# A two-block float32 network on one core: the first projection fed by blocks of 128 channels, seven units at once

## The reference

```python
c_act = jax.nn.silu(c)
mod = c_act @ ada_w[l] + ada_b[l]                 # [1, 6*1024]
sh1, sc1, g1, sh2, sc2, g2 = split(mod, 6)
h = rmsnorm(x, norm_mix_w[l]) * (1.0 + sc1) + sh1 # [512, 1024]
proj = h @ w_in[l]                                # [512, 3624]
(hq, hf, hi, hg, sq, sk, sv, iq, ik, iw, cu) = split(proj)
o_a = hgrn2_mixer(hq, hf, hi, hg, ...)            # recurrence over chunks
o_b = dsa_mixer(sq, sk, sv, iq, ik, iw)           # scores of iq, ik, iw; top 128 keys; attention
o_c = conv_module(cu, ...)                        # gate, convolution of 31 taps, layer norm
x = x + g1 * (concat(o_a, o_b, o_c) @ w_out[l])
```

## Time and profile before

| | us |
|---|---|
| median of three runs | 1356.24 |
| the profiled execution's own time | 1354.19 |
| its span | 1352.6 |
| PE busy | 1278.8 (95%) |
| DVE busy | 849.5 (63%) |
| ACT busy | 579.9 (43%) |
| POOL busy | 103.9 (8%) |
| mean granted clock of PE | 0.974 |

### The profile page before, as it was taken

The page is one execution under the profiler, slowest core; times in us unless marked ns, Lnnn a source line. Parts: engine busy times, 40 slices in busy tenths (PEclk is TensorE's granted clock), DMA queues, the critical chain, the costliest instruction groups (busy, mean ns, idle before and its releaser), DMA issues.

```text
span 1352.6 us, 18764 instructions
## 1 busy us (share of the span) xinstructions
PE 1278.8 (95%) x6581; PEld 1026.4 (76%) x6581; DVE 849.5 (63%) x1273; ACT 579.9 (43%) x820; POOL 103.9 (8%) x154
## 2 busy tenths in 40 slices
PE   6799788999899999999999999999999989999997
PEld 2677566878688788788888888787788877777776
DVE  4679798666765422344444787775366547887853
ACT  3366442651444211244333465332233335878731
POOL 7014330000000000000000000110011000000000
PEclk9799898998899999999999999999999999999999
DMA  8576982323544433333333223333222332333231
GB/s 295 149 209 134 201 167 70 111 78 124 157 140 132 132 93 93 86 101 93 93 93 94 69 87 86 90 91 106 84 87 81 98 93 70 87 90 92 59 94 62
DMA packets 209912, 147.88 MB, mean 109 GB/s; under 512 B 7682, under 2 KB 192177, under 8 KB 209856
## 3 DMA queue, kind: packets, MB, share of 16 engines
q1 hardware_dynamic: 200784, 134.40, 33.6%
q0 software_dynamic: 6848, 11.69, 4.9%
q10 hardware_dynamic: 2224, 1.05, 0.3%
HBM read 135.06 MB, written 2.10 MB: 101 GB/s over the span
## 4 chain that ended last, share of the span: by engine, by line
PE 69%; DVE 14%; issue 6%; DMA 5%; ACT 5%; POOL 1%; DVEq 0%; ACTq 0%; SPq 0%; POOLq 0%
PE banks L393 21%; PE banks L395 20%; PE banks L394 20%; ACT w_hi L365 2%; DVE w_lo L377 2%; DMA raw<-in_ada_w 1%; DMA cacc<-rstd 1%; DMA cacc<-sqb 1%; DVE score L1812 1%; POOL e L2513 1%; DVE score L1829 1%; DVE m L1826 1%; DVE vh L2221 1%; DMA omix<-rstd 1%; DVE hgt L1790 1%
## 5 line engine op out<-in xcount | busy, mean ns | idle before, releaser
L393 PE MATMUL banks<-h_hi,w_hi 128*128 128x512 f32 x824 | 332.6, 404 | 13.7 <-issue 4.7
L377 DVE TENSOR_TENSOR w_lo<-raw,w_hi 128x1024 fp32r<-128x1024 f32 x204 | 250.3, 1231 | 150.3 <-ACT w_hi L365 145.8
L394 PE MATMUL banks<-h_lo,w_hi 128*128 128x512 f32 x824 | 324.5, 394 | 0.0
L395 PE MATMUL banks<-h_hi,w_lo 128*128 128x512 f32 x824 | 324.1, 393 | 0.0
L365 ACT ACTIVATE w_hi<-raw 128x1024 fp32r<-128x1024 f32 x204 | 213.5, 1050 | 162.0 <-PE banks L395 143.8
L393 PEld LDWEIGHTS banks<-h_hi,w_hi 128*128 128x128 f32 x824 | 157.1, 191 | 54.8 <-issue 13.6
L394 PEld LDWEIGHTS banks<-h_lo,w_hi 128*128 128x128 f32 x824 | 157.2, 191 | 34.2 <-issue 2.6
L395 PEld LDWEIGHTS banks<-h_hi,w_lo 128*128 128x128 f32 x824 | 156.9, 190 | 33.7
L393 PE MATMUL banks<-n_hi,w_hi 128*128 128x512 f32 x256 | 102.5, 400 | 2.9 <-DVE h_lo L2266 1.7
L393 PE MATMUL banks<-hid_hi,w_hi 128*128 128x512 f32 x256 | 102.0, 398 | 0.0
L394 PE MATMUL banks<-hid_lo,w_hi 128*128 128x512 f32 x256 | 101.7, 397 | 0.0
(11 more groups left out here) (381 smaller groups left out, 1849.2 us busy)
## 6 DMA issues: line engine op xcount, KB each, us to landing
raw<-in_mlp_w SPq DMA_DIRECT2D x64, 512.0 KB, 4.1
raw<-in_a_w_in SPq DMA_DIRECT2D x48, 512.0 KB, 3.9
raw<-in_ada_w SPq DMA_DIRECT2D x40, 512.0 KB, 4.5
raw<-in_w_in SPq DMA_DIRECT2D x28, 512.0 KB, 4.5
raw<-in_b_w_in SPq DMA_DIRECT2D x24, 512.0 KB, 3.8
raw<-in_a_w_out SPq DMA_DIRECT2D x16, 512.0 KB, 4.0
raw<-in_b_w_out SPq DMA_DIRECT2D x16, 384.0 KB, 3.4
raw<-in_w_out SPq DMA_DIRECT2D x8, 512.0 KB, 4.4
```

What stands on the lines that cost most here:

```text
L377: dve.tensor_tensor(dst, src, hi, ALU.subtract).then_inc(split_lo, 1)
L393: pe.matmul(dst, l_hi, r_hi, start=first, stop=False)
L394: pe.matmul(dst, l_hi, r_lo, start=False, stop=False)
L395: return pe.matmul(dst, l_lo, r_hi, start=False, stop=last)
```

## The change

It feeds the first seven products k-tile by k-tile. `STREAM` begins with eight groups of four loads: a block of `ada_w` for the scale of 128 channels ("block", 1, k), one for the shift ("block", 0, k), the 128 rows of `w_in` for all seven front units at once ("w", k; 896 columns in four pieces), and a row tile of group 2 ("rows", 2, k). PE multiplies the scale block itself (`scale_column`), DVE multiplies and reduces the shift block (`shift_products`, `shift_sum`) and PE sums over partitions (`shift_column`). A `front_step(k)` is 21 matmuls: seven banks by three. The sums of squares are taken per token on `x_tok` before it is turned. All six groups of scores come behind units HQ and later, and the tables of side work are drawn anew; unit numbers of what follows the front grow by one.

```diff
-ADA_PE = [ada_unit(1, k) for k in range(KT)]
-ADA_DVE = [ada_unit(g, k) for g in (0, 2, 4, 3) for k in range(KT)]
-STREAM = [t for k in range(KT) for t in (ADA_PE[k], ADA_DVE[k])] + [("w", u) for u in range(LEAD)]
+ADA_PE = [("block", 1, k) for k in range(KT)]
+ADA_SHIFT = [("block", 0, k) for k in range(KT)]
+ADA_DVE = [("rows", g, k) for g in (2, 4, 3) for k in range(KT)]
+STREAM = [t for k in range(KT) for t in (ADA_PE[k], ADA_SHIFT[k], ("w", k), ADA_DVE[k])]
...
-ROUNDS_AT = {6: [(1,)] * 3, 7: [(1,)] * 3, 8: [(1, 2)], ...
+ROUNDS_AT = {10: [(1,)] * 2, 11: [(1,)] * 2, 12: [(1,)], ...
...
-PRODUCTS_AT = {5: 2, 6: 3, 7: 3, 8: 2, 9: 2, 10: 2, 11: 2, 12: 3, 13: 3, ...
+PRODUCTS_AT = {9: 3, 10: 3, 11: 3, 12: 3, 13: 3, 14: 3, 15: 3, 16: 3, ...
...
+            def scale_column(k):
+                d = arrival[ADA_PE[k]]
+                raw_wait(pe, d)
...
+                    pe.wait_ge(mod_ready, k)
+                for t in range(KT):
+                    last = pe.matmul(banks[:, COLUMN_BANK, k:k + 1], raw[:, d % RING, t * P:(t + 1) * P], c_act[:, t:t + 1],
+                                     start=(t == 0), stop=(t == KT - 1))
+                last.then_inc(ada_used, 1)
...
+            def front_step(k):
+                pe.wait_ge(split_lo, k + 1)
+                pe.wait_ge(h_ready, H_MIX + k + 1)
...
+                for n, bank in enumerate(FRONT_BANKS):
+                    if n == 3 and k + 1 < KT:
+                        shift_column(k + 1)
+                    last = three(pe, banks[:, bank, :], w[:, n, :], w0[:, n, :], h_hi[:, k, :], h_lo[:, k, :], k == 0, k == KT - 1)
+                last.then_inc(w_used, 1)
...
+            for k in range(KT):
+                if k + 1 < KT:
+                    scale_column(k + 1)
+                front_step(k)
...
+            for k in range(KT):
+                dve.wait_ge(ada_used, k + 1)
+                dve.wait_ge(mod_summed, k + 1)
+                scaled = chain.step(dve.scalar_tensor_tensor(scale1[:, k:k + 1], banks[:, COLUMN_BANK, k:k + 1], sc1[:, k:k + 1],
+                                                             pcol("norm_mix_w", k), ALU.add, ALU.mult))
+                dve.tensor_tensor(mod[:, k:k + 1], banks[:, COLUMN_BANK, KT + k:KT + k + 1], pcol("ada_b", k), ALU.add)\
+                   .then_inc(mod_ready, 1)
...
+                dve.scalar_tensor_tensor(sqb[:, k % 2, :], xT[:, k, :], scale1[:, k:k + 1], rstd[:, :], ALU.mult, ALU.mult)\
+                   .then_inc(h_scaled, 1)
+                if k + 1 < KT:
+                    dve.wait_ge(shift_summed, k + 1)
+                    shift_products(k + 1)
...
+                if k + 1 < KT:
+                    shift_sum(k + 1)
+                ada_tile(k)
+                lo_unit(dve, k + 1)
```

More of the change, by code:

```diff
@@ L40 @@
 UNIT = 1024
-def ada_unit(group, kt):
-    return ("ada", group, kt)
 W_IN_UNITS = (
-    [("fm", C_IQ), ("fm", C_IQ + P), ("ikw", C_IK)]
-    + [("fm", C_CU + P * m + CV * s) for m in range(CVT) for s in range(2)]
+    [("front", k) for k in range(KT)]
     + [("fm", C_HQ + P * h) for h in range(HG_HEADS)]
@@ L462, in _ @@
                         sp.wait_ge(ada_used, ADA_PE.index(before) + 1)
+                    elif before in ADA_SHIFT:
+                        sp.wait_ge(shift_read, ADA_SHIFT.index(before) + 1)
                     else:
@@ L689, in scores @@
                     r = slice(IDX_D * h, IDX_D * (h + 1))
-                    last = pe.matmul(banks[:, 4 + h, 0:P * (b + 1)], iqT[r, half, b * P:(b + 1) * P], ikT[r, 0:P * (b + 1)],
-                                     start=True, stop=True)
+                    c0 = 2 * P * half if b == 1 else 0
+                    dst = banks[:, 4 + h, c0:c0 + P * (b + 1)]
+                    last = pe.matmul(dst, iqT[r, half, b * P:(b + 1) * P], ikT[r, 0:P * (b + 1)], start=True, stop=True)
                 last.then_inc(s_made, 1)
@@ L1070, in _ @@
             stat_columns(Q_AO + KT)
-            spread(rs, 6, 4)
+            spread(rs, 6, 5)
             pe.wait_ge(x_new, X_BO)
@@ L1212, in _ @@
-            for u in range(LEAD):
-                hi_unit(act, u)
-            act.wait_ge(mod_ready, 2)
-            shifted(0, 0)
+            plain_wait()
+            chain.link(act.activation(junk[:, :], eps_c[:, 0:1], ACT.Sqrt))
+            for m in range(KT):
+                act.wait_ge(x_turned, m + 1)
+                act.activation(xT[:, m, :], banks[:, 4 + m % 4, :], ACT.Copy).then_inc(x_new, 1)
+                if m == 5:
+                    act.wait_ge(x_squared, TT)
+                    act.activation(rs[:, :], rs1[:, :], ACT.Sqrt, bias=eps_c[:, 0:1]).then_inc(root_made, 1)
@@ new lines, in _ @@
+            chain.link(act.activation(junk[:, :], eps_c[:, 0:1], ACT.Sigmoid))
+            hi_unit(act, KT + 1)
+            hi_unit(act, KT + 2)
+            act.wait_ge(w_used, KT)
+            for n in range(2):
+                act.activation(iqT[:, n, :], banks[:, FRONT_BANKS[n], :], ACT.Copy).then_inc(evac, 1)
+            ikw = FRONT_BANKS[2]
+            act.activation(ikT[0:3 * IDX_D, :], banks[0:3 * IDX_D, ikw, :], ACT.Copy)
+            act.activation(ikT[3 * IDX_D:, :], banks[0:IDX_D, ikw, :], ACT.Copy)
@@ L1217, in read_out @@
+            act.activation(iwT, banks[3 * IDX_D:, ikw, :], ACT.Copy, scale=float(IDX_HEADS * IDX_D) ** -0.5).then_inc(evac, 1)
+            for m in range(CVT):
+                act.activation(hpad[:, m, TAPS - 1:], banks[:, FRONT_BANKS[3 + m], :], ACT.Copy).then_inc(evac, 1)
+                act.activation(cacc[:, m, :], banks[:, FRONT_BANKS[3 + CVT + m], :], ACT.Sigmoid).then_inc(evac, 1)
             def read_out(u):
@@ L1433, in _ @@
             done = 0
-            for u in range(N_IN):
+            for u in range(U_HQ, N_IN):
                 hi_unit(act, u + LEAD)
```

422 lines of the change are left out of this document (206 added, 216 removed).

## The result

The changed kernel takes **1387.8 us** in the median of 4 runs, the kernel before 1356.0 in runs beside it: ratio 1.0258, 95% interval 1.0231 to 1.0285. It is slower, as forecast, and just inside the range, but by 31.7 us and not by 14.6. The profiled execution took 1388.2 (span 1386.6, before 1352.6).

What follows compares the result with a forecast made beforehand. The prediction took PE, busy for 95% of the span, as the bound of most of the kernel, untouched by the change. Front +6.6, middle -3 and attention's slots +11 gave +14.6 us, so 1371 us, range 1348 to 1388.

Steps and rivals of the forecast that it cites:

- The loop of releases: Front: SP's in-order queue holds the next blocks behind the row tile, which waits for DVE's release; this sets each pass.
- The size of the pass: Front: one pass takes 6.4 + 4.1 = 10.5 to 10.6 us, with bounds 9.4 and 11.3.
- Landing: Front, each pass: the third block is there 6.3 to 6.5 us after the release, with loads at 406 to 413 GB/s.
- The bound of 340 GB/s: Front: loads at the mean of the busy slices, near 340 GB/s, give the upper bound of a pass, 11.3 us.
- Shift sum: Front, DVE in each pass: a reduction over 1024 elements, taken at the 1024-wide subtraction's 1.1 us; upper bound twice that.
- the last step: End of front: 3.5 us to h, then 21 products taken at 6.5 us, between 4.8 and 9.0.
- the first release: Start of the front's loop: DVE's first row tile operation is done and releases the next loads at 27.6 us.
- PE at the half clock in every step: Rival, front: PE bounds a pass at 13.0 us, the kernel takes 1388 us; chance 0.12.
- The middle: End of front to join of the taps: 127 us, between 121 and 131, against 129.8 before: -3 us.
- The give-back of the moved rounds: Middle: rounds put behind the join take 11.1 us of DVE work out of the stretch ahead of it.
- The attention's slots: Behind the join: moved rounds add 12.5 us of DVE work, of which 1.5 is hidden: +11 us.
- other side: Rival, front: the loop runs at the engines' work, a pass is PE's 6.9 us, the kernel takes 1347 us; chance 0.18.

Runs made afterwards that it cites:

- Experiment 6: The changed kernel with every scale and shift block loaded as a row tile of the same size (scale and shift wrong): ratio 1.0223 to the kernel before.
- experiment 5: The changed kernel with `w_in` slices behind the first cut to 16 columns in each piece: ratio 1.0252 to the kernel before.
- Experiment 2: The changed kernel with the shift sum replaced by a copy of its first 128 columns (shift not computed): ratio 1.0183 to the kernel before.
- experiment 11: The changed kernel with the shift sum taken over eight neighbouring elements (wrong numbers): 1379.9 us in one run, beside 1353.0 of the kernel before.
- experiment 1: The changed kernel with scale and shift blocks of a k-tile loaded ahead of the row tile of the k-tile before: ratio 1.0066 to the kernel before.
- experiment 7: The changed kernel with the edits of experiment 1 and experiment 4 joined (blocks ahead, early rounds): ratio 1.0003 to the kernel before.
- experiment 3: The kernel before with the changed kernel's table of rounds, one slot number lower (late rounds): ratio 1.0042 to the kernel before.
- experiment 4: The changed kernel with three double and three single rounds moved ahead of the join: ratio 1.0221 to the kernel before.
- experiment 9: Experiment 7 with the eight row tiles loaded and used behind the front, in DVE's first slots: ratio 1.0016 to the kernel before.
- Experiment 10: Experiment 9 with the first scores added ahead of their slot's row tiles and one tile a slot later: ratio 0.9981 to the kernel before.
- experiment 8: Experiment 7 with two rounds and two third taps more at slot 9: ratio 1.0019 to the kernel before.

## Why the prediction was right in sign and too small

**The mechanism of the pass: right.** The loop of releases through SP's queue was named, with its releaser: DVE waits for a DMA of `ada_w` in each pass, SP issues three loads 0.02 us behind the row tile's operation, and the one line that moves the row tile behind the blocks takes 21 us out of the front.

**The size of the pass: the step that failed.** "A pass is therefore 6.4 + 4.1 = 10.5 to 10.6 us" measured 7.7 + 4.9 = 12.6. Over six passes that is 12 of the 19.4 us by which the span grew beyond the forecast (34.0 against 14.6). Two terms of it were short.
- *Landing, 6.4 against 7.7.* I took the best slices, 406 to 413 GB/s, from a stretch in which row tiles alone are loaded; the blocks' pieces of 512 bytes run near 310. Experiment 6 gives 0.7 us for the pieces, and some 0.4 more goes with rows of 4 KB that ran below my rate as well; the slice of weights, the other suspect, gives nothing (experiment 5). The bound of 340 GB/s was not wide enough. The Trainium skill's limit of 358 GB/s (the section that the prediction named) would have been nearer than my 406 to 413: even rows of 4 KB ran at 360 to 375 in a pass.
- *Shift sum, 1.1 against 1.9.* It reads 1024 elements with a step of 128 elements between neighbours, and I priced it as an elementwise operation of that width; my upper bound, twice the value, held it. Experiment 2 gives its whole price per pass, and experiment 11 says that the stride is most of what I missed: with neighbours it takes 1.21, close to my 1.1.

Six passes of 2.0 us more are 12; the last step was 1.3 us shorter than forecast (103.4 to 112.1, 8.7 against 10.0), the first release as forecast (27.8 against 27.6). Sum +10.9: the front's error. The first release was in part luck: in the profiled executions of experiments 1, 2 and 7 the shift products of k = 1 begin at 26.9 to 27.0, in the other nine with the new front at 22.3 to 23.4.

**The clock.** The rival "PE at the half clock in every step" forecast 1388 us, near the measured time, but not by its mechanism. Rows of the changed kernel show products 0.42 apart behind a wait (101.06 to 101.48) and 0.23 apart behind work in a row (107.59 to 107.82), so the 1.2 GHz level came back in every pass, as the Trainium skill (TensorE: Matmul & The Clock Gate, section HAM oscillation) describes. But PE had idle time in each pass, and with shorter waits (experiment 1) the clock rose without any other change.

**The middle: -3 forecast, +0.8 measured.** DVE's work was 113.0 us against 111.9 forecast, its idle time 17.6 against 15. The give-back of the moved rounds is 7.6 us and not the 11.1 of their work.

**The attention's slots: +11 forecast, +15.7 measured.** The rounds themselves cost 11.2 to 12.1 (experiments 3 and 4), DVE's work there grew by 11.3. The rest, some 4 us, goes with the granted clock: 0.87 in that stretch against 0.94 in experiment 3, which has the same rounds, 90.0 us and 75.0 us of PE work in place of 94.4 and 80.3. Busy us behind the join, experiment 3, then experiments 9 and 10:

```profile
216.70:306.70 90.00, 75.02 (x487) 62.64 (x487) 66.11 (x151) 40.19 (x77) 0.58 (x2) 0.94 0.27 82
```
```profile
220.40:303.00 82.60, 77.97 (x514) 65.52 (x514) 54.85 (x123) 39.54 (x76) 0.59 (x2) 0.93 0.30 90
```
```profile
218.10:294.80 76.70, 72.12 (x492) 60.56 (x493) 54.84 (x123) 39.54 (x76) 0.58 (x2) 0.98 0.32 97
```

Experiments 9 and 10 have the same instructions behind the join, and still the stretch takes 82.6 us at a clock of 0.93 and 76.7 at 0.98. So 4 us is within what the clock makes of one and the same code from one execution to another; what sets it there stays open, and each of these is one execution.

**The "other side".** That a pass at the engines' own work would be much faster than before was wrong in its sum, too: with a pass of 6.9 us and late rounds I had 1347. Experiment 10 has such passes (6.6 to 7.1 us from 39.20 on) and early rounds as well, and its median is 1349.9. As long as DVE waits in the front, the join follows the front's end: from 112.1 to 91.2 (experiment 1) it moved by the whole 21.0 us. Below that DVE's own work holds it: experiment 10 ends its front 15.2 us ahead of the kernel before, and from there to the join DVE works for 132.0 of 138.7 us. Counted from the start, DVE is idle for 18.7 us less than before but has 12.5 us more to do, so the join gains 6.2.

## What to carry to other kernels

In a ring with one queue, the order of loads is an order of releases: put a load whose slot comes free late behind those whose slots come free early, or every load waits for the latest. Price a loop of releases from rows with the same shape of transfer, since each microsecond of error counts once per pass. And before you rebuild a stretch in which one engine is full, look at what the other engines did beside it: here DVE's side work moved behind the front and grew by 12 us, so even a front 15 us shorter brought the join only 4 to 6 us forward.

## What the runs showed of the hardware

On DVE, 1024 elements read 128 elements apart cost 0.7 us more than neighbours (1.92 against 1.21), and written 8 elements apart 0.9 us more (2.09 against 1.23). The Trainium skill (SBUF — State Buffer, section "Door 1: The DMA port swizzle") says that accesses that cross from one line of 16 bytes to the next pay a penalty; the four numbers agree in direction. A DVE operation can also take longer beside GpSimd's: in experiment 10 the low part of a weights' tile took 3.50 us where its kind takes 1.23, with POOL operations of 0.96 and 1.94 us inside it. The Trainium skill (the same page, section Terms) has the two engines share one pair of ports that one of them holds for a whole instruction; the 2.3 us more are about what POOL's two cover together (100.04 to 102.24), but by the rows DVE's operation began 0.2 us ahead of them and was the one that took longer, so who held the ports is not shown, and no run here tried it apart. DVE's row and POOL's:

```profile
99.83 3.50 DVE L373 TENSOR_TENSOR w_lo<-raw,w_hi 128x1024 fp32r<-128x1024 f32 x1 [0.18 <-ACT w_hi L367]
```
```profile
100.04 0.96 POOL L2527 TENSOR_SCALAR_AFFINE_SELECT score<-score 128x128 f32<-128x128 f32 x1
100.30 1.94 POOL L2540 TENSOR_TENSOR hq<-hq,hk 128x512 f32<-128x512 f32 x1
```

And the start of the front varies from execution to execution: the first scale column, the same 16 records, took 1.84 us in one profile (experiment 8) and 3.41 in another (experiment 7), where the shift products of k = 1 began at 22.6 and at 26.9 us. The recorded granted clock doesn't tell the two apart, it is 1.00 from 8 to 20 us in both; why the products ran at half the rate in one stays open.
